# Ten of twelve groups of a convolution mixer's input projection computed token-stationary, and a re-timed exchange through memory

## What is computed

```python
def causal_dwconv(u, w):
    K = w.shape[0]
    T = u.shape[1]
    up = jnp.pad(u, ((0, 0), (K - 1, 0), (0, 0)))
    return sum(up[:, k:k + T] * w[k] for k in range(K))

def short_conv_mixer(xn, w_in, conv_w, w_out):
    """y = W_out( B * conv3( C * h ) ), [B, C, h] = W_in x."""
    proj = xn @ w_in
    gb, gc, h = jnp.split(proj, 3, axis=-1)
    y = gb * causal_dwconv(gc * h, conv_w)
    return y @ w_out

def conv_glu_ffn(xn, w_up, conv_w, w_down):
    u = causal_dwconv(xn @ w_up, conv_w)
    gate, val = jnp.split(u, 2, axis=-1)
    return (jax.nn.silu(gate) * val) @ w_down
```

## Time and profile before

| | |
|---|---|
| median of 3 runs | 2313.37 us (2310.45 to 2316.09) |
| profiled execution | 2307.13 us |
| its span, first to last instruction | 2305.3 us |
| TensorE's mean granted clock | 0.999 |
| SC_IN, from its first product to SC_OUT's | 1219.15 to 1487.64 us |
| UP0 and UP1, the same way | 496.88 to 976.54 and 1576.71 to 2057.63 us |

### The profile page before, as it was taken

The page is one execution under the profiler, slowest core; times in us unless marked ns, Lnnn a source line. Parts: engine busy times, 40 slices in busy tenths (PEclk is TensorE's granted clock), DMA queues, the critical chain, the costliest instruction groups (busy, mean ns, idle before and its releaser), DMA issues.

```text
span 2305.3 us, 33959 instructions
## 1 busy us (share of the span) xinstructions
PE 2293.1 (99%) x11430; PEld 1933.5 (84%) x11430; DVE 1687.8 (73%) x2132; ACT 1061.4 (46%) x1109; POOL 2.8 (0%) x9
## 2 busy tenths in 40 slices
PE   9999999999999999999999999999999999999998
PEld 8888888888888888888888888888888888878887
DVE  7979889867878878865556676666878878876544
ACT  7444444554444444444445444444444444444443
POOL 0000000000000000000000000000000000000000
PEclk9999999999999999999999999999999999999999
DMA  7555555567887888876665656556887887887764
GB/s 246 167 176 163 174 168 167 174 200 229 240 246 230 247 238 238 238 226 191 190 192 184 192 186 191 184 192 202 236 246 237 245 237 230 244 247 215 230 192 156
DMA packets 388936, 483.10 MB, mean 210 GB/s; under 512 B 17904, under 2 KB 243568, under 8 KB 388720
## 3 DMA queue, kind: packets, MB, share of 16 engines
q1 hardware_dynamic: 387840, 479.52, 68.5%
q10 hardware_dynamic: 1008, 2.43, 0.3%
HBM read 454.61 MB, written 25.17 MB: 208 GB/s over the span
## 4 chain that ended last, share of the span: by engine, by line
PE 82%; DVE 9%; issue 5%; DMA 3%; ACT 1%; SPq 1%; DVEq 0%; ACTq 0%
PE acc L1414 18%; PE acc L1415 18%; PE acc L1416 18%; PE acc L1348 17%; PE acc L1358 9%; DVE w_parts L728 2%; DMA raw<-in_ffn_w_up 1%; DMA moved<-crossing 1%; DVE a_diag L1048 1%; DVE fpre L1033 1%; DVE kl L1015 1%; DVE tb L890 1%; DVE ta L890 1%; ACT w_parts L450 1%; PE side L1519 0%
## 5 line engine op out<-in xcount | busy, mean ns | idle before, releaser
L450 ACT ACTIVATE w_parts<-raw 128x1024 fp32r<-128x1024 f32 x815 | 860.0, 1059 | 1043.9 <-PE acc L1416 513.4
L728 DVE TENSOR_TENSOR w_parts<-raw,w_parts 128x1024 fp32r<-128x1024 f32 x816 | 984.5, 1223 | 477.5 <-ACT w_parts L450 285.7
L1414 PE MATMUL acc<-w_parts,xn 128*128 128x512 f32 x1408 | 549.1, 390 | 1.0 <-DVE w_parts L728 1.0
L1415 PE MATMUL acc<-w_parts,xn 128*128 128x512 f32 x1408 | 548.2, 389 | 0.0
L1416 PE MATMUL acc<-w_parts,xn 128*128 128x512 f32 x1408 | 548.2, 389 | 0.0
L1348 PE MATMUL acc<-xn,w_parts 128*128 128x512 f32 x1536 | 368.7, 392 | 1.4 <-ACT w_parts L450 0.7
L1348 PEld LDWEIGHTS acc<-xn,w_parts 128*128 128x128 f32 x1536 | 282.3, 188 | 57.1 <-DVE xn L784 1.2
L1414 PEld LDWEIGHTS acc<-w_parts,xn 128*128 128x128 f32 x1408 | 264.5, 188 | 57.3 <-DVE w_parts L728 2.7
L1416 PEld LDWEIGHTS acc<-w_parts,xn 128*128 128x128 f32 x1408 | 264.5, 188 | 55.1
L1415 PEld LDWEIGHTS acc<-w_parts,xn 128*128 128x128 f32 x1408 | 264.5, 188 | 54.1
L1414 PE MATMUL acc<-w_parts,act 128*128 128x512 f32 x704 | 274.6, 390 | 0.5 <-DVE w_parts L728 0.5
(11 more groups left out here) (152 smaller groups left out, 1265.1 us busy)
## 6 DMA issues: line engine op xcount, KB each, us to landing
raw<-in_ffn_w_up SPq DMA_DIRECT2D x352, 512.0 KB, 3.9
raw<-in_ffn_w_down SPq DMA_DIRECT2D x176, 512.0 KB, 4.6
raw<-in_hgrn_w_in SPq DMA_DIRECT2D x127, 512.0 KB, 3.9
raw<-in_sc_w_in SPq DMA_DIRECT2D x96, 512.0 KB, 4.4
crossing<-turned SPq DMA_DIRECT2D x44, 512.0 KB, 3.4
moved<-crossing SPq DMA_DIRECT2D x176, 128.0 KB, 4.6
raw<-in_hgrn_w_out SPq DMA_DIRECT2D x32, 512.0 KB, 3.5
raw<-in_sc_w_out SPq DMA_DIRECT2D x32, 512.0 KB, 4.7
```

Of the source, the lines that this page charges most:

```text
L450: nc.scalar.activation(w_parts[:, c % RING, :, 0, :], raw[:, c % RING], ACT.Copy).then_inc(hi_ready, 1)
L728: v.tensor_tensor(w_parts[:, c % RING, :, 1, :], raw[:, c % RING], w_parts[:, c % RING, :, 0, :].bitcast(F32), ALU.subtract).then_inc(lo_r ...
L1414: mm(bank, x_hi, hi, start=begin and q == 0, stop=False)
L1415: low = mm(bank, x_hi, lo, start=False, stop=False)
```

## The change

Ten of SC_IN's twelve groups become token-stationary and use the exchange of the up projections. The last two (h and B of the last set of tiles) stay feature-stationary, as a phase of their own, SC_LAST. The conv steps of the ten groups are spread over the steps of the groups behind them (`conv_steps`). For the up projections too, the fetch moves one weight load ahead on SP (10 to 9), and scaling, taps, product and result parts each move one step later on VectorE. In DOWN1 one turn of the residual and the stores behind it move by one step.

```diff
--- before.py
+++ after.py
@@ -102,8 +102,9 @@
 HGRN_OUT = Phase(HGRN_IN, 2, 2, DT)
 UP0 = Phase(HGRN_OUT, 11, 2, DT, scales=2, corrects=False, parts=1)
 DOWN0 = Phase(UP0, 2, 2, FT, corrects=False, parts=1)
-SC_IN = Phase(DOWN0, 2, 6, DT, scales=6)
-SC_OUT = Phase(SC_IN, 2, 2, DT, corrects=False)
+SC_IN = Phase(DOWN0, 1, 10, DT, scales=10, corrects=False, parts=1)
+SC_LAST = Phase(SC_IN, 1, 2, DT, scales=2)
+SC_OUT = Phase(SC_LAST, 2, 2, DT, corrects=False)
 UP1 = Phase(SC_OUT, 11, 2, DT, scales=2, corrects=False, parts=1)
 DOWN1 = Phase(UP1, 2, 2, FT, corrects=False, parts=1)
 CHUNKS = DOWN1.c0 + DOWN1.n * DOWN1.cpi
@@ -137,12 +138,12 @@
 S_RS_SC = S_DOWN + DT // TG
 S_RS_UP1, S_H = S_RS_SC + 1, S_RS_SC + 2
 QUARTER = P // 4
-TURN_H_AT = [8, 12, 19, 26]
-MOVE_H_AT = [17, 21, 28, 36]
-
-
-STORED_AT, FETCHED_AT = 7, 10
-SCALED_AT, CONV_AT, PRODUCT_AT, SPLIT_HIGH_AT, SPLIT_LOW_AT = 4, 5, 8, 9, 10
+TURN_H_AT = [9, 12, 19, 26]
+MOVE_H_AT = [18, 21, 28, 36]
+
+
+STORED_AT, FETCHED_AT = 7, 9
+SCALED_AT, CONV_AT, PRODUCT_AT, SPLIT_HIGH_AT, SPLIT_LOW_AT = 5, 6, 9, 10, 11
 
 
 def loop(e, phase, body, peel_last=False):
@@ -306,7 +307,7 @@
 
         y_tok = h[:].rearrange("p j t -> p (j t)").rearrange("p (b n) -> p b n", b=T // P)
 
-        turned_groups = {UP0: 0, UP1: UP0.n * UP0.groups}
+        turned_groups = {UP0: 0, SC_IN: UP0.n * UP0.groups, UP1: UP0.n * UP0.groups + SC_IN.groups}
 
         block = ctx.enter_context(nc.Block())
 
@@ -368,16 +369,21 @@
                 if step == FETCHED_AT:
                     fetch_moved(i, up, 1)
 
-            def stream(phase, w, column, up=None):
+            def cross_conv(g, kk):
+
+                if kk == STORED_AT and 0 < g <= SC_IN.groups:
+                    store_turned(0, SC_IN, g - 1)
+                if kk == FETCHED_AT - SC_IN.cpg and g > 1:
+                    fetch_moved(0, SC_IN, g - 2)
+
+            def stream(phase, w, column, ahead=None):
 
                 def body(i, first):
                     for g in range(phase.groups):
                         for kk, (part, k, _, _) in enumerate(phase.steps(first, g)):
                             c = phase.c0 + g * phase.cpg + kk
-                            if phase is up:
-                                cross(i, first, g, kk, up)
-                            elif up and first:
-                                cross_last(up.n - 1, g * phase.cpg + kk, up)
+                            if ahead:
+                                ahead(i, first, g, kk)
                             if first and phase is HGRN_IN and g == 0 and kk in X_LOADED_BEFORE:
                                 load_x(X_LOADED_BEFORE[kk])
                             if first and phase is HGRN_IN and (g, kk) == (0, LATE_PARAMETERS_BEFORE):
@@ -416,12 +422,19 @@
             sp.dma_start(h[:, 0:TW, :], x[:, 0:TW, :]).then_inc(first_x_loaded, 16)
             stream(HGRN_IN, hgrn_w_in[0], lambda i, g: i * GC + [D, 0, 2 * D, 3 * D][g])
             stream(HGRN_OUT, hgrn_w_out[0], lambda i, g: i * (2 * GC) + g * GC)
-            stream(UP0, ffn_w_up[0], lambda i, g: i * GC + g * FF, UP0)
-            stream(DOWN0, ffn_w_down[0], lambda i, g: i * (2 * GC) + g * GC, UP0)
-            stream(SC_IN, sc_w_in[0], lambda i, g: i * (2 * GC) + (g // 3) * GC + [D, 2 * D, 0][g % 3])
+            stream(UP0, ffn_w_up[0], lambda i, g: i * GC + g * FF,
+                   lambda i, first, g, kk: cross(i, first, g, kk, UP0))
+            stream(DOWN0, ffn_w_down[0], lambda i, g: i * (2 * GC) + g * GC,
+                   lambda i, first, g, kk: cross_last(UP0.n - 1, g * DOWN0.cpg + kk, UP0) if first else None)
+            stream(SC_IN, sc_w_in[0], lambda i, g: g // 3 * GC + [D, 2 * D, 0][g % 3],
+                   lambda i, first, g, kk: cross_conv(g, kk))
+            stream(SC_LAST, sc_w_in[0], lambda i, g: 3 * GC + [2 * D, 0][g],
+                   lambda i, first, g, kk: cross_conv(SC_IN.groups + g, kk))
             stream(SC_OUT, sc_w_out[0], lambda i, g: i * (2 * GC) + g * GC)
-            stream(UP1, ffn_w_up[1], lambda i, g: i * GC + g * FF, UP1)
-            stream(DOWN1, ffn_w_down[1], lambda i, g: i * (2 * GC) + g * GC, UP1)
+            stream(UP1, ffn_w_up[1], lambda i, g: i * GC + g * FF,
+                   lambda i, first, g, kk: cross(i, first, g, kk, UP1))
+            stream(DOWN1, ffn_w_down[1], lambda i, g: i * (2 * GC) + g * GC,
+                   lambda i, first, g, kk: cross_last(UP1.n - 1, g * DOWN1.cpg + kk, UP1) if first else None)
             y = out[0].rearrange("(b p) n -> p b n", p=P)
             for b in range(T // P):
                 sp.wait_ge(y_tok_ready, b + 1)
@@ -634,6 +647,7 @@
                 if first and (g, kk) == (0, RS_AT):
                     root(3)
             phase_of(SC_IN, sc)
+            phase_of(SC_LAST, lambda i, first, g, kk: None)
             residual_phase(SC_OUT, 16, NORM_FFN + DT)
             up_phase(UP1, UP0.n, 4)
 
@@ -873,23 +887,23 @@
                                 rs[:, 0:T].rearrange("p (s t) -> p s t", t=QUARTER)[:, :, None, :].to_broadcast(by_block),
                                 ALU.mult).then_inc(scaled_ready, 1)
 
+            def tap(dst, column, step, n):
+
+                for j in range(TG):
+                    w = par[:, bass.ds(column + n * step + j, 1)]
+                    src = pad[:, j, n:n + T]
+                    if n == TAPS - 1:
+                        o = v.tensor_scalar(dst[:, j, :], src, w, None, ALU.mult)
+                    else:
+                        o = v.scalar_tensor_tensor(out=dst[:, j, :], in0=src, scalar=w, in1=dst[:, j, :],
+                                                   op0=ALU.mult, op1=ALU.add)
+                return o
+
             def up_phase(phase, n, rs_n, rs_stage, conv):
 
                 late_links = 7
                 late_base = late[0]
                 u = pad[:, :, TAPS - 1:]
-
-                def tap(dst, column, n):
-
-                    for j in range(TG):
-                        w = par[:, bass.ds(column + n * 2 * FT + j, 1)]
-                        src = pad[:, j, n:n + T]
-                        if n == TAPS - 1:
-                            o = v.tensor_scalar(dst[:, j, :], src, w, None, ALU.mult)
-                        else:
-                            o = v.scalar_tensor_tensor(out=dst[:, j, :], in0=src, scalar=w, in1=dst[:, j, :],
-                                                       op0=ALU.mult, op1=ALU.add)
-                    return o
 
                 def late_steps(i, step):
 
@@ -905,7 +919,7 @@
                         if n_tap == TAPS - 1:
                             late[1] = 0
                             await_scaled(i, phase, 0)
-                        o = tap(ta, conv + i * TG, n_tap)
+                        o = tap(ta, conv + i * TG, 2 * FT, n_tap)
                         if n_tap:
                             late_link(o)
                         else:
@@ -916,7 +930,7 @@
                         n_tap = TAPS - 1 - (step - CONV_AT)
                         if n_tap == TAPS - 1:
                             await_scaled(i, phase, 1)
-                        late_link(tap(tb, conv + FT + i * TG, n_tap))
+                        late_link(tap(tb, conv + FT + i * TG, 2 * FT, n_tap))
                     if step == PRODUCT_AT:
                         dve.wait_ge(silu_ready, at(i, 1, n + 1))
                         late_link(v.tensor_tensor(tb[:], ta[:], tb[:], ALU.mult))
@@ -1215,25 +1229,55 @@
                     fold_squares(3)
                 if first and (g, kk) == (0, RS_AT):
                     rms(3, S_RS_SC)
-                tile = i * (2 * TG) + (g // 3) * TG
-                if g % 3 == 2 and kk == 0:
+                conv_steps(g - 1, kk)
+                conv_steps(g - 2, kk + SC_IN.cpg)
+
+            def conv_steps(g, step):
+
+                if not 0 <= g < SC_IN.groups:
+                    return
+                kind, tile = g % 3, g // 3 * TG
+                u = pad[:, :, TAPS - 1:]
+                dst = act[:, tile:tile + TG, :, :]
+                if step == SCALED_AT:
+                    scaled_moved(0, SC_IN, g, u if kind == 1 else ta[:])
+                if step == SCALED_AT + 1 and kind:
+                    await_scaled(0, SC_IN, g)
+                    if kind == 1:
+                        link(v.tensor_tensor(u, u, ta[:], ALU.mult), 0)
+                    else:
+                        link(v.tensor_tensor(tb[:], ta[:], tb[:], ALU.mult), 0)
+                if kind == 1 and 2 <= step - SCALED_AT < 2 + TAPS:
+                    link(tap(tb, SC_CONV + tile, DT, TAPS + 1 - (step - SCALED_AT)), 0)
+                if kind == 2 and step == SCALED_AT + 2:
+                    link(v.tensor_copy(dst[:, :, 0, :], tb[:]), 0)
+                if kind == 2 and step == SCALED_AT + 3:
+                    v.tensor_tensor(dst[:, :, 1, :], tb[:], dst[:, :, 0, :].bitcast(F32), ALU.subtract) \
+                        .then_inc(act_ready, 1)
+
```

(25 more changed lines are left out.)

## The result

The changed kernel takes **2299.43 us** (median of 4 runs, 2298.80 to 2300.04), against 2314.45 us for the kernel before (4 runs, 2310.45 to 2316.09): 15.0 us less, a ratio of 0.994 with a 95% interval of 0.9925 to 0.9955, clear of 1 but under 1%. The forecast was 2307.8 us and a ratio of 0.9976.

A forecast was written before the change was run, and what follows sets the result against it. The kernel was taken as bound by the spacing of TensorE's products. Terms of -5.1 + 0.3 - 0.8 = -5.6 us, taken from the median of 2313.37, gave 2307.8 us, with a range of 2303.5 to 2312.5 us.

The forecast's parts named there:

- The mixer's stage: SC_IN: 80 chunks turned token-stationary save 0.063 us each; with 0.1 us less waiting, -5.1 us.
- the rival of an unchanged pace: Mixer's stage: token-stationary chunks run no faster on its operands, leaving only 0.5 us of moves, 2312.9 us; chance 0.03.
- The exchange in the new stage: SC_IN's ten groups: added transfers and VectorE work cost 0 to 1.0 us, taken as +0.3 us.
- the first rival: Mixer's new stage: 28% more traffic and bunched loads make weights late, leaving -3.1 us, 2310.3 us; chance 0.25.
- The up projections: UP0 and UP1: sooner fetch and later scaling nearly end VectorE's waits, giving back 0 to 2.5 us, taken as -0.8 us.
- the stalls above: UP0 and UP1 in the profiled execution: stalls and one summing of squares cost 1.0 us and 2.2 us.
- The gain spent on late weights: Mixer's new stage: 28% more traffic, loads bunching behind the four fetches, leaves -3.1 us, 2310.3 us; chance 0.25.
- The SiLU gate: Up projections: a later last tap holds ScalarE and its weight splits, 0.5 us stall in 22 iterations, 2319.6 us; chance 0.07.
- the 4 us of margin: Up projections: ScalarE's split after the SiLU gate is done by 2027.7, its chunk due at 2031.8, leaving 4 us.

The follow-up runs named there:

- narrow_lows: The kernel before with the new timing, SC_IN's 256-column products cut into two of 128: the stage takes 349.65 us, 81.2 longer.
- conv_only: The changed kernel with the old timing of fetch and steps, so the mixer's new form alone: 2306.56 us, ratio 0.9967 to before.
- before_again: The kernel before, unchanged, profiled a second time: this execution took 2318.34 us.
- no_wait: The kernel before, all transfers kept, but the up projections' scaling reads a resident tile of h instead of the fetched one: 2303.99 us, ratio 0.9970.
- fetch_only: The kernel before with only the fetch one weight load sooner on SP (10 to 9), VectorE's steps unmoved: 2304.33 us, ratio 0.9963.
- steps_only: The kernel before with only VectorE's steps one chunk later, the fetch staying at 10: 2304.39 us, ratio 0.9962.
- fetch_later: The kernel before with only the fetch moved later, 10 to 11, VectorE's steps unmoved: 2415.11 us, ratio 1.0423.
- both_later: The kernel before with the fetch at 11 and VectorE's steps one later, keeping their distance of 6: 2320.14 us, ratio 1.0023.

## Why the prediction was right in part and wrong in size

**The mixer's stage: right.** Forecast 263.4 to 263.6 us, measured 263.47 or 263.48 in all four kernels with it. The pace of 226.7 ns held on this stage's operands, so the rival of an unchanged pace is out. Of the other price, 120 ns for half a width, `narrow_lows` shows that it lies 7 to 10 ns above a floor of 110 to 113.

By the formula that the prediction took from the Trainium skill ("TensorE: Matmul & The Clock Gate", "Back-to-back issue gap") the stage would have gained 0.8 us. The measured 5.0 us stand by the rows' 120 and 227 ns and not by the formula's 109 and 216. The prediction left out what that section says beside it: the formula is the gap of an isolated product, and for a stream of loads and products, which this kernel is, the section gives about 131 ns for 512 columns and 81 for 128. The rows here, 227 and 110 to 113 ns, agree with neither.

**The exchange in the new stage: right, at the favourable end.** I took 0.3 us of the 0 to 1.0. TensorE does not wait, with DMA at 82% and 232 GB/s (forecast 78% and 235). The 28% more traffic of the first rival was misread: 188 to 241 GB/s is a rate, and the stage's bytes grow by 21%, ten groups of 1.05 MB on 96 chunks of 0.52 MB. And even with the old timing in `conv_only` the stage takes 263.47 us. VectorE has 31% to spare there (180.88 of 263.50 us busy), and in UP1 20%.

**The up projections: the step that failed.** "What this can give back is at most the stalls above: 0 to 2.5 us ... I take -0.8 us, a third of the stalls." In the place of 0.8 the new timing measured 8.1 us by the medians, a term off by a factor of ten. The stages' floor was sized well enough (479.2 where I had 478.7 and a summing of squares). What failed was taking the stalls of one execution as the bound of all. The sign stood in the prediction itself: "The median of the runs lies 6.2 us above that execution, for no reason that the trace shows". The reason was the very wait that the same prediction priced: `before_again` has nearly all of its surplus in UP0, UP1 and DOWN0, and in `no_wait` it is gone. Against the floor of 2304.3 us without waits, before's median of 2313 us has 9 us of stalls, and the profiled execution had 3.

**How the wait works, which I had in words but not as a loop.** I wrote that the waits "made VectorE late with splits, and through `lo_ready` they made SP late with loads", and stopped there. It closes. SP issues each load when VectorE has split an earlier chunk. A late VectorE also turns its group late: in the earlier trace rows the turned group is stored at 2018.53. Counting two chunks back from ScalarE's release by TensorE at 2018.2, the group had ended at 2012.8, so the store comes 5.7 us after it. In the changed kernel ScalarE's split is released at 2012.98 and the store stands at 2009.72, 2.2 us after the group's end at 2007.54, and VectorE scales with no wait:

```profile
1993.16 1.84 SPq L353 DMA_DIRECT2D moved<-crossing  x4
...
2009.72 0.37 SPq L346 DMA_DIRECT2D crossing<-turned  x1
```

```profile
2004.33 1.22 DVE L885 TENSOR_TENSOR pad<-moved,rs 128x1024 f32<-128x1024 f32 x1
...
2008.38 1.31 DVE L874 STREAM_TRANSPOSE turned<-acc 128x512 f32<-128x512 f32 x2 [0.19 <-DVE ta L896]
```

```profile
2007.54 1.06 ACT L463 ACTIVATE w_parts<-raw 128x1024 fp32r<-128x1024 f32 x1 [1.66 <-PE acc L1460]
...
2012.98 1.07 ACT L463 ACTIVATE w_parts<-raw 128x1024 fp32r<-128x1024 f32 x1 [1.66 <-PE acc L1460]
```

A late store makes a late fetch, which makes the next wait. The same four transfers, issued from 1993.16 on, have 11 us here before VectorE comes for them, against a median landing of 4.5 us. `fetch_only` cuts the loop at SP's end, `steps_only` at VectorE's, `no_wait` cuts VectorE's wait alone, and each gets the whole 8 us. The slip of the fetch behind TensorE (8.8 us at UP1's start, up to 15.3 later, against 10.8 at most without the wait) is the loop itself; `fetch_later` strengthens it and loses 101 us.

**The gain spent on late weights: wrong.** It was given 0.25. Neither TensorE nor VectorE waits for the added traffic. Nor does SP's place behind a store matter, for `fetch_only` reaches the floor.

**The SiLU gate: it exists, and does not decide.** ScalarE's wait rose from 10.6 to 18.8 us (I had said perhaps 30) with no wait of TensorE behind it. My margin was wrong, though: the split released at 2018.2 follows the end of the *second* chunk, so the group ended at 2012.8 and not 2015.5, and the 4 us of margin were 1.4. That the rival stayed away because VectorE was no longer late is an argument and not measured; in `both_later`, where VectorE was late, the gate's 73.7 us came along with 6 us.

**What stays open.** Why one execution of the old kernel has 3 us of stalls and another 14 was not found. The same transfers may land somewhat sooner or later and the loop enlarge that, but no run varied it on purpose. How much of the gate's wait costs time was not separated, nor what bounds a narrow product. The last two feature-stationary groups and the other feature-stationary stages were not tried in the token-stationary form.

## What to carry to other kernels

When the profiled execution is faster than every other run shown beside it, its stalls are too low a measure. Take the stages' lengths without waits from the products' spacing, subtract them from the median, and ask which wait the rest is. A wait off the critical path is not free when the waiting engine also paces the queue that it waits for: such a wait can feed itself. Here one step of slack, on SP's side or on VectorE's, was worth as much as removing the wait, while one step less cost 101 us. The scatter was a sign too: several us with the waits, about 1 us in every kernel without them.

## What the runs showed of the hardware that I had not expected

With one stationary load of 128 x 128 for each product, products of 128, 256 and 512 columns stand 110 to 113, 120 and 227 ns apart at a granted clock of 0.999 (`narrow_lows` and the earlier trace rows): below 256 columns a product gets hardly cheaper. And in the changed kernel's UP1 the DMA engines move 238 GB/s, 84% busy, for 479 us without one wait of TensorE, though of the run's 54 stores single ones took up to 9.0 us to land where the median was 3.8:

```profile
DMA to landing us min/median/max: 3.3/3.8/9.0
```
